# Norm scales for all 512 columns at once: sums by a full matrix of ones, root and reciprocal over 512 columns

## The reference

```python
def _rmsnorm(x, g):
    xf = x.astype(jnp.float32)
    y = xf * lax.rsqrt(jnp.mean(xf * xf, axis=-1, keepdims=True) + RMS_EPS)
    return (y * g.astype(jnp.float32)).astype(x.dtype)

# first block, one layer
h = h + FFN_HALF * _swiglu(_rmsnorm(h, norm_ffn1), ffn1_gate, ffn1_up, ffn1_down)   # norm 0
u = _rmsnorm(h, norm_mix)                                                          # norm 1
...                                                    # projections, two attention branches, merge
h = h + FFN_HALF * _swiglu(_rmsnorm(h, norm_ffn2), ffn2_gate, ffn2_up, ffn2_down)   # norm 2
x = _rmsnorm(h, norm_final)                                                        # norm 3
# second block, two layers l = 0, 1
h = rms_norm(x, norm_w[l])                                                         # norms 4 and 5
x = x + hybrid_mixer(h, ...)
return rms_norm(x, final_norm_w)                                                   # norm 6
```

## Time and profile before

| | |
|---|---|
| median of three runs | 2531.38 us |
| the profiled execution, its own time | 2532.64 us |
| its span in the trace | 2531.2 us |
| PE busy | 2383.6 us (94% of the span) |
| DVE busy | 1065.1 us (42%) |
| ACT busy | 926.2 us (37%) |
| POOL busy | 869.5 us (34%) |
| mean granted TensorE clock | 0.964 of full |

### The profile page before, as it was taken

One profiled execution on the slowest core, in us unless ns is written; L12 is line 12 of the kernel. 1 busy time (PEld: TensorE's weight loads), 2 busy tenths in 40 slices (PEclk: granted clock), 3 DMA queues, 4 the chain that ended last, 5 costly groups with the idle time before them and its releaser, 6 DMA issues.

```text
span 2531.2 us, 29492 instructions
## 1 busy us (share of the span) xinstructions
PE 2383.6 (94%) x12132; PEld 1958.0 (77%) x12132; DVE 1065.1 (42%) x1799; ACT 926.2 (37%) x1538; POOL 869.5 (34%) x424
## 2 busy tenths in 40 slices
PE   5999998989999999999998999999898999999898
PEld 4888786776665777887876778998686778899687
DVE  3000123745555521000226875654333876665232
ACT  3222233224344533222233553444523473444432
POOL 2444443411011234444433542222243452222242
PEclk9999998979999999999997999999998999999998
DMA  4222222210001122322221210000121220000122
GB/s 153 93 99 100 88 96 96 83 38 26 26 26 42 67 84 75 100 94 98 92 92 45 83 56 26 26 26 30 67 96 67 86 81 18 26 26 26 51 99 75
DMA packets 46197, 169.41 MB, mean 67 GB/s; under 512 B 5232, under 2 KB 6000, under 8 KB 45808
## 3 DMA queue, kind: packets, MB, share of 16 engines
q1 hardware_dynamic: 45344, 165.73, 19.3%
q10 hardware_dynamic: 720, 1.79, 0.2%
HBM read 165.40 MB, written 2.10 MB: 66 GB/s over the span
## 4 chain that ended last, share of the span: by engine, by line
PE 84%; DVE 9%; ACT 5%; issue 1%; DMA 0%; POOL 0%; ACTq 0%; DVEq 0%
PE ps L305 21%; PE ps L307 20%; PE ps L306 20%; PE ps L696 4%; PE ps L704 3%; PE ps L693 2%; PE ps L485 2%; PE ps L451 2%; PE ps L566 1%; DVE rt L1205 1%; PE ps L466 1%; PE ps L322 1%; DVE xl L1209 1%; PE ps L395 1%; ACT dl L1133 1%
## 5 line engine op out<-in xcount | busy, mean ns | idle before, releaser
L1659 POOL TENSOR_TENSOR wlo<-raw,whi 128x1024 fp32r<-128x1024 f32 x300 | 731.2, 2438 | 1287.5 <-ACT whi L771 1287.5
L305 PE MATMUL ps<-xh,whi 128*128 128x512 f32 x1728 | 717.2, 415 | 54.4 <-POOL xl L1667 18.5
L307 PE MATMUL ps<-xh,wlo 128*128 128x512 f32 x1728 | 683.8, 396 | 0.0
L306 PE MATMUL ps<-xl,whi 128*128 128x512 f32 x1728 | 683.4, 395 | 0.0
L305 PEld LDWEIGHTS ps<-xh,whi 128*128 128x128 f32 x1728 | 331.3, 192 | 158.6 <-issue 38.9
L771 ACT CAST whi<-raw 128x1024 fp32r<-128x1024 f32 x300 | 313.8, 1047 | 275.4 <-DMA raw<-in_stream 200.0
L307 PEld LDWEIGHTS ps<-xh,wlo 128*128 128x128 f32 x1728 | 330.4, 191 | 71.6
L306 PEld LDWEIGHTS ps<-xl,whi 128*128 128x128 f32 x1728 | 332.1, 192 | 64.9 <-issue 5.0
L1241 DVE TENSOR_TENSOR mid<-sil,ps 128x512 f32<-128x512 f32 x44 | 30.3, 688 | 443.3 <-PE ps L307 439.7
L1441 DVE SCALAR_TENSOR_TENSOR cu<-up,lcols,cu 128x512 f32<-128x512 f32 x180 | 166.4, 944 | 0.7
L1684 POOL TENSOR_TENSOR cu<-cu,prod 128x512 f32<-128x512 f32 x60 | 81.0, 1349 | 208.9 <-ACT prod L970 208.7
(11 more groups left out here) (286 smaller groups left out, 3312.3 us busy)
## 6 DMA issues: line engine op xcount, KB each, us to landing
raw<-in_stream SPq DMA_DIRECT2D x300, 512.0 KB, 3.2
w1k<-in_w SPq DMA_DIRECT2D x1, 2048.0 KB, 16.2
w1v<-in_w SPq DMA_DIRECT2D x1, 2048.0 KB, 8.3
outT<-h SPq DMA_DIRECT2D x4, 512.0 KB, 2.7
h<-in_xT ACTq DMA_DIRECT2D x2, 512.0 KB, 6.5
h<-in_xT SPq DMA_DIRECT2D x2, 512.0 KB, 6.0
mats<-in_mats ACTq DMA_DIRECT2D x1, 448.0 KB, 10.5
msk<-in_masks SPq DMA_DIRECT2D x1, 258.0 KB, 12.2
```

Of the source, the lines that this page charges most:

```text
L305: pe.matmul(out, wh, hi, start=first, stop=False)
L306: pe.matmul(out, wh, lo, start=False, stop=False)
L307: return pe.matmul(out, wl, hi, start=False, stop=last)
L1659: pool.tensor_tensor(m.wlo[:, slot, :], m.raw[:, slot, :], m.whi[:, slot, :].bitcast(F32), ALU.subtract).then_inc(s.wlo)
```

## The change

In each of the seven norms, the sums of squares are now made by one matmul for a pair, with the 128x128 matrix of ones as weights and the 512 columns of squares as the moving side. The sum of a column then stands in all 128 partitions at once, in `ps[:, 6, :]`. ACT takes the root of 128x512 from there into `ps[:, 5, :]`, DVE the reciprocal of 128x512 in place, and `spread`, its buffer `scl` and its semaphore go. DVE's multiplication now waits for DVE's own reciprocal.

```diff
-    def token_sums(out, squares, first, last):
-        for j in range(NT):
-            ins = pe.matmul(out[:, j:j + 1], squares[:, j * P:(j + 1) * P], mat(m, "ones")[:, 0:1],
-                            start=first and j == 0, stop=last, skip_group_check=True)
-        return ins
-
-    def spread(out, colsum):
-        for j in range(NT):
-            ins = pe.matmul(out[:, j * P:(j + 1) * P], colsum[:, j:j + 1].broadcast_to([P, P]), ident,
-                            start=True, stop=True)
-        return ins
-
     def norm(e):
         for n in range(4):
             pe.wait_ge(s.pair, 4 * e + n + 1)
-            token_sums(ps[:, 6, 0:NT], m.rt[:, (2 * n + 1) % 4, :], n == 0, n == 3).then_inc(s.sums)
-        pe.wait_ge(s.scale, e + 1)
-        spread(ps[:, 5, :], m.scl[:, 0:NT]).then_inc(s.spread)
+            pe.matmul(ps[:, 6, :], mat(m, "ones"), m.rt[:, (2 * n + 1) % 4, :], start=n == 0, stop=n == 3).then_inc(s.sums)
...
     def root(e):
         act.wait_ge(s.sums, 4 * e + 4)
-        act.activation(m.scl[:, 0:NT], ps[:, 6, 0:NT], ACT.Sqrt, bias=eps, scale=1.0 / D).then_inc(s.root)
+        act.activation(ps[:, 5, :], ps[:, 6, :], ACT.Sqrt, bias=eps, scale=1.0 / D).then_inc(s.root)
...
     def norm_scale(e):
         dve.wait_ge(s.root, e + 1)
-        dve.reciprocal(m.scl[:, 0:NT], m.scl[:, 0:NT]).then_inc(s.scale)
-        dve.wait_ge(s.spread, e + 1)
+        dve.reciprocal(ps[:, 5, :], ps[:, 5, :]).then_inc(s.scale)
+        dve.wait_ge(s.scale, e + 1)
```

More of the change, by code:

```diff
@@ L142 @@
 SIGNALS = (
[L143 to L150, removed]
+    "wlo xl_even xl_odd unit pair sums mid ml xr rope rot kc2 vxr vturn blk z1 cmp1 in_mix hidden cmp2 kc_raw "
+    "kc_rot in_w1v kcc vtok vc_raw gate_row cmask expd score probs pt0 pt1 ptc turned o_new pv cw cturn vcc "
+    "gts cscore ysum mix_lo h_new yl up wab_lo ab qconv ab_raw ab_t sq_qkv ab_read decay sums_qkv l2 gl cum "
+    "cum_s filled conv shared mean o_sq o_sums cu_sq var o_dn d_snew d_vns d_pre d_kk d_onew d_qk d_qd d_at "
+    "d_a d_t d_u d_ys d_y d_att d_us d_uy d_ttk d_ttv d_kd d_kc d_vt d_kcs d_s0 d_vn d_s d_q d_o in_par raw0 "
+    "raw1 raw2 raw3 whi in_h0 in_h1 in_h2 in_h3 square root y xh angle trig sil mh poly tanh gts_sig negmax "
+    "csub cexp mix_hi sg yh prod glu_sig zero qkv log_qkv root_qkv soft_dve soft_act d_eg cum_d d_exp z_used "
+    "cu_c o_log log_cu o_root root_cu cu_n cu_silu d_neg d_min d_dec eps dve_step scale in_pos d_t0 h_out "
     "wab_hi out_dma "
```

## The result

The changed kernel takes 2538.14 us as the median of twelve runs, beside 2531.33 for the kernel before: a ratio of 1.0027, with a 95% interval of 1.0019 to 1.0036. That is 6.8 us slower (4.8 to 9.1). The forecast was 11.6 us, with a range of 2535.5 to 2550. The direction and the range held; the size was too large by some 5 us.

What follows compares the result with a forecast made beforehand. The prediction took TensorE to bound the kernel, with 84% of the chain of waits. 10.2 us from root to multiplication plus 1.4 from sum to root made 11.6, so 2543.0 us, 0.46% slower; range 2535.5 to 2550.

Steps and rivals of the forecast that it cites:

- The chain: Each norm is a serial chain; a microsecond more or less in it moves everything behind it.
- From root to multiplication: Root's start to DVE's first multiplication: 4.11 us in place of 2.65, 1.46 more in each norm, 10.2 in seven.
- Rivals A and B: Wide reciprocal in each norm: A, flows at 0.69 us, 2524.3, 6%; B, eight passes a column, 4.3 us, 2549.5, 12%.
- From sum to root: Sum's start to root's start: 2.1 us in place of 1.90 at the lower clock, 1.4 us more over the norms.
- rival C: PE's clock stays up through the norms' sums: 8.6 us less, 2534.4; half way 2539, 14% from there down.
- What hides the rest: Behind each norm PE waits for x, up to 14.4 us after the first multiplication in norm 1; nothing hides the shift.
- Rival D: PE idles through root and reciprocal, so the clock comes back later behind norms: 3 us more, 2546, 6%.
- E: The chain isn't what ends last; part of the shift is taken up elsewhere, so time moves by under 5 us; 2%.
- The span and the time: Whole kernel: span from 2531.2 to 2542.8 us, median from 2531.38 to 2543.0, 11.6 us slower.
- The signs: Profile after: seven reciprocals at 3.2 to 3.5 us, roots 0.6 to 0.7, sum to root 2.0 to 2.3 in norm 1.

Runs made afterwards that it cites:

- the cut reciprocal: Changed kernel with the root fed a scale of zero and the reciprocal covering 32 columns into an unread buffer, division left out: 2518.10 us, ratio 0.9953.
- the single operation: Changed kernel with root and reciprocal replaced by one absolute reciprocal square root on ACT: 2510.33 us, ratio 0.9921.
- the sums alone: Changed kernel with the reciprocal cut to 280 columns, tail as long as the old one, division left out: 2526.24 us, ratio 0.9986.
- the two mirror experiments: Kernel before with wide matmuls added between its sums: 2549.42 us, ratio 1.0065; changed kernel with short matmuls added between its sums: 2556.76 us, ratio 1.0103.

## Why the prediction was right in direction and too large

- **The chain**: right. Every change of a norm's length came through, within 1 to 3 us of the whole (the cut reciprocal 21 by the trace and 19 to 20 by the medians, the single operation 23.8 and 27, the sums alone 5.6 and 5.7).
- **From root to multiplication**: right. 4.11 forecast, 4.09 to 4.10 measured in all seven norms. The extrapolation from 4 and 32 columns gave 3.37 for the reciprocal, and it took 3366 to 3367 ns; 280 columns took 1917 ns. The 0.66 for the root, taken from a logarithm of the same shape, was 662 ns. 10.2 us in seven, as in the sum. Rivals A and B are out: neither a flow at 0.69 nor eight steps for a column.
- **From sum to root**: this term was mis-sized, in its sign too. I priced the new sums at the lower clock since the old ones ran there: 1.4 us more. They took 5.6 us less, because the clock is up for the last sum: 1.21 to 1.35 from the last pair to the root in the place of 1.96 to 2.63. 10.2 - 5.6 is the 4.6 of the table. I had this as rival C with 14%, and dismissed it with the words that PE would be busy under half of the time, as before. The profile has it otherwise: it counts PE busy in 81% of the stretch from the first sum of norm 1 to its root before, in 99% after, and in 99 and 100% in the two mirror experiments, where the clock was low at the last sum (the windows in the last section). So PE's busy time doesn't tell these cases apart. C in full would have been 7.2 us off the old sums; it came to 5.6, and half of what is missing is norm 4, which gained 0.7 and not 1.5.
- **The mechanism behind C**: not quite as I put it. The clock doesn't simply stay up. In norms 1 and 3 it falls in the pause behind the stage before and comes back within the sums (at 415.1 in norm 1), in norm 4 it falls while PE idles behind norm 3 and comes back ahead of the last sum; in 2, 5 and 6 it stays up until the sums are over. "Moving columns hold it" is too simple as well, since more columns between the old sums left it low in five of six. What the runs show is that the low clock at the last sum goes with batches of weight loads with one moving column: in all six norms before, in five of six with wide matmuls added, in three of six where they stand between wide sums, and in none with wide sums alone. Norm 0 sorts all twelve traces: in the seven with wide sums alone full clock is first on record 18.6 to 20.5 us into the span, within the sums; in the five with short ones among them not before 33.7 to 40.3, in the stage behind. Nor is it the moment of the fall. In norm 3 the clock falls at 1323.2 before and at 1323.1 after, in both just ahead of the first sum, and is back at 1329.9 after, but only at 1357.3 before, behind norm 4. A window of it, before and then after:

```profile
1330.00:1331.00 1.00, 1.00 (x6) 1.00 (x6) 0.00 (x0) 0.14 (x1) 0.00 (x0) 0.50 0.00 0
```
```profile
1330.00:1331.00 1.00, 0.91 (x2) 0.08 (x1) 0.00 (x0) 0.28 (x2) 0.00 (x0) 1.00 0.00 0
```

  What exactly the chip weighs stays open: no run tells whether the short matmuls pull the clock down, or only lengthen the time over which the columns of the wide ones are spread. TensorE: Matmul & The Clock Gate of the Trainium skill says in Part 1 that the gate goes by how busy the PE has been. Busy as the profile counts it, the shares above don't bear that out.
- **What hides the rest**: right. The clock behind a norm costs nothing (14.43 us with PE kept busy, 14.44 without). Rival D is out, and E too, as the cut reciprocal and the single operation show.
- **The span and the time**: the traces put 4.6 and 4.8 us on the norms, the runs say 6.8 (4.8 to 9.1) and 6.1 (3.8 to 8.1). The dense stages between the norms, whose instructions are the same, aren't equally long in every trace. The last layer, from the last wait for x to the last matmul ahead of norm 6, took 561.2 and 559.7 us in the two traces of the kernel before, 563.2 and 563.2 in those of the changed one. All twelve traces sort by their sums, whatever stands behind them: the last layer took 559.7 to 561.2 us in the four with the old sums, and 562.4 to 563.8 in the eight with the new ones. The clock stood at 1.2 GHz for 13.7 to 17.1 us of it in the four, for 17.1 to 23.9 in the eight. Two windows where they differ, second trace of the kernel before first, then the changed kernel's first trace:

```profile
2090.00:2110.00 20.00, 15.47 (x111) 14.39 (x109) 15.19 (x20) 5.55 (x8) 6.30 (x4) 0.91 0.00 1
2160.00:2180.00 20.00, 17.38 (x136) 16.06 (x134) 16.03 (x24) 7.98 (x12) 5.00 (x4) 1.00 0.08 27
```
```profile
2090.00:2110.00 20.00, 15.47 (x105) 14.38 (x103) 14.61 (x19) 5.17 (x8) 7.11 (x5) 0.83 0.00 1
2160.00:2180.00 20.00, 17.38 (x117) 15.86 (x117) 14.97 (x23) 6.27 (x11) 3.26 (x4) 0.91 0.08 27
```

  The granted clock is 0.83 and 0.91 in these where it was 0.91 and 1.00. Against that, the stage between norms 4 and 5 took 563.1 and 563.3 before and 562.8 and 562.7 after, but 559.8 with the single operation. Why the clock falls at other places inside a stage when the norm ahead of it has changed isn't settled; it would take up the 1 to 2 us between the traces and the runs.
- **The signs**: most of them came as written (the reciprocals, the roots, no spreading, the same stretch from root to multiplication in all seven norms, the clock back before the last wait for x). DVE was busy for 18 and 24 us more in the two pairs of traces, where 22 was expected. Two spoke against the forecast: the 1.2 for C, and a stage between two norms that changed its length, as the last layer did.
- **Luck**: the norms alone put 4.6 to 4.8 us on the kernel, under half of the 11.6. They would give some 2536 us, just inside the range. That the runs came nearer to the forecast is owed to some 2 us in the dense stages, where it had put nothing.

## What to carry to other kernels

Where a short result feeds a wide one (a root, a reciprocal of some numbers for all partitions), ask of each operation what a column costs before widening it: ACT's root took 0.40 us more for the 512 columns and the wide sums saved time, but DVE's reciprocal, at 6.3 ns a column, cost 3.2 us more and ate the whole gain. And where a chain runs over a PE that otherwise waits, price PE's part for the form that it has after the change: the clock that the old form saw is not the clock that the new one gets.

## What was unexpected of the hardware

- TensorE's clock in a thin stretch doesn't follow from PE's busy time in the profile. The windows from norm 1's first sum to its root, before and after (PE and PEld busy are the first two times behind the length, PEclk stands behind the five engines):

```profile
409.50:417.40 7.90, 6.42 (x32) 6.08 (x32) 5.06 (x8) 4.40 (x6) 0.00 (x0) 0.65 0.60 250
```
```profile
408.70:416.10 7.40, 7.32 (x8) 1.93 (x8) 5.05 (x8) 4.21 (x6) 0.00 (x0) 0.57 0.60 254
```

  PE counts as busy for most of both, and the mean clock is even lower in the second; what differs is the weight loads, 6.08 against 1.93, and where the clock is up: at the start of the stretch before, at its end after, where the last sum is waited for. The same stretch with wide matmuls between the old sums, and with short ones between the new:

```profile
412.90:422.90 10.00, 9.87 (x38) 7.45 (x38) 5.08 (x8) 4.40 (x6) 0.00 (x0) 0.62 0.46 194
```
```profile
416.00:428.30 12.30, 12.30 (x32) 7.63 (x32) 5.01 (x8) 4.21 (x6) 0.00 (x0) 0.50 0.38 159
```

  PE has hardly a gap in them, and the clock was at 1.2 GHz at the last sum of both; in the second it stayed there for 27 us.
- ACT's absolute reciprocal square root costs 662 ns for 128x512 in PSUM, the same as its square root or its logarithm, and the load of its table, 1.28 us, is as well covered: 3.4 us a norm less than root and reciprocal on two engines.
- A reciprocal on DVE takes the same 6.3 ns a column in PSUM (1917 ns for 280 columns, 3367 for 512) as in SBUF (178 for 4, 354 for 32), while a scalar operation of 512 columns took 0.75 us from PSUM against 0.43 in SBUF.
